# One f32 product in place of three f32r products in an encoder layer's projection, with the sample's experts chosen for both tiles together and the prompt's input normed beside it

## What is computed

```python
h = rmsnorm(x, g_mix)
proj  = h @ w_in                    # 3072 columns: q, k, v of branches A and B
gates = sigmoid(h @ w_gate + b_gate)   # 2048 columns
# A: windowed attention, 16 heads of 64;  B: dense attention, 8 heads of 128, q and k normed, rotary
x = x + (ga * (oa @ w_oa) + gb * (ob @ w_ob)) @ w_out
h = rmsnorm(x, g_ffn)               # then, for each token, 8 heads of:
qry = h @ w_query                   # 2 halves of 128 a head
s_top, i_top = top_k(qry . sub_keys, 16)       # for each half, over 128 keys
best, pos = top_k(s_top[0][:, None] + s_top[1][None, :], 16)
idx = i_top[0] * 128 + i_top[1] at pos;  g = softmax(best)
x = x + sum over the 128 chosen of  g * gelu(u[idx] . h) * v[idx]    # u, v: 16384 experts
y = rmsnorm(x, g_final)
```

## Time and profile before

| | us |
|---|---|
| median of 3 runs | 4944.76 (4940.06 to 4950.62) |
| the profiled execution, its time | 4939.81 |
| the profiled execution, span from first to last instruction | 4937.9 |
| PE busy, PEld | 3098.5 (63%), 1782.3 (36%) |
| DVE busy, ACT, POOL | 3340.8 (68%), 1042.4 (21%), 1728.8 (35%) |
| mean granted clock of TensorE | 0.739 |
| moved by DMA | 1568.77 MB, 318 GB/s |

### The profile page before, as it was taken

How to read it: one execution, slowest core, us unless ns; L and a number is a source line. 1 busy time by engine, 2 the same in 40 slices (tenths; PEclk the granted TensorE clock), 3 DMA queues, 4 the chain that set the end, 5 groups by cost and what they waited for, 6 DMA issues and landing times.

```text
span 4937.9 us, 72225 instructions
## 1 busy us (share of the span) xinstructions
PE 3098.5 (63%) x27052; PEld 1782.3 (36%) x27052; DVE 3340.8 (68%) x7744; ACT 1042.4 (21%) x2853; POOL 1728.8 (35%) x1393
## 2 busy tenths in 40 slices
PE   7686389885999989955545455445455444454433
PEld 6545367663777744432212112122122122121000
DVE  4426777786888866658867767667667577677554
ACT  3311111221555521111121121111211211211111
POOL 0200033323344323224444444444444444444443
PEclk9897699987999999966656666666566566565555
DMA  6143288897445477689999999999999999999998
GB/s 238 62 165 113 95 325 330 330 341 283 165 150 190 156 310 280 245 315 385 389 401 393 393 404 394 389 404 403 406 389 389 402 392 392 394 391 383 407 392 326
DMA packets 281852, 1568.77 MB, mean 318 GB/s; under 512 B 28064, under 2 KB 48032, under 8 KB 112928
## 3 DMA queue, kind: packets, MB, share of 16 engines
q0 software_dynamic: 184320, 1342.26, 68.9%
q1 hardware_dynamic: 97184, 221.90, 12.1%
...
## 4 chain that ended last, share of the span: by engine, by line
DMA 32%; issue 7%; PE 7%; DVE 5%; POOL 4%; ACT 2%; another core or an unknown queue 0%; POOLq 0%; DVEq 0%; SPq 0%; ACTq 0%
DMA prompt_exp_ring<-in_experts_dram,prompt_exp_idx 29%; PE prompt_exp_acc L1966 6%; POOL prompt_exp_ring L1619 4%; DVE prompt_exp_junk L1864 3%; DMA prompt_exp_ring<-in_experts_dram,prompt_exp_idx_all 3%; ACT prompt_exp_diag L1696 2%; PE prompt_exp_qp L1927 1%; DVE prompt_exp_pos L1743 0%; DVE prompt_exp_best L1739 0%; PE prompt_exp_qp L1987 0%; DVE prompt_exp_dot L1864 0%; DMA prompt_exp_wq<-in_w_query_dram 0%; DVE prompt_exp_crest L1748 0%; DVE prompt_exp_topi L1743 0%
## 5 line engine op out<-in xcount | busy, mean ns | idle before, releaser
L1966 PE MATMUL prompt_exp_acc<-prompt_exp_ring,prompt_exp_diag 32*32 32x512 f32 x16384 | 936.3, 940 | 1396.1 <-ACT prompt_exp_diag L1696 1395.3
L1864 DVE CUSTOM_DVE_ANT_0 prompt_exp_junk<-prompt_exp_ring,prompt_exp_h_now 128x1024 bf16<-128x1024 f32 x1024 | 1244.9, 1227 | 698.3 <-DMA prompt_exp_ring<-in_experts_dram,prompt_exp_idx 654.0
L1619 POOL DMA_INDIRECT prompt_exp_ring<-in_experts_dram,prompt_exp_idx x896 | 1032.0, 1152 | 1369.8 <-PE prompt_exp_acc L1966 1205.3
L1966 PEld LDWEIGHTS prompt_exp_acc<-prompt_exp_ring,prompt_exp_diag 32*32 32x32 f32 x16384 | 168.6, 127 | 1948.6 <-issue 1945.9
L1690 ACT ACTIVATE prompt_exp_ge<-prompt_exp_dot 128x2 f32<-128x2 f32 x512 | 104.1, 203 | 2286.8 <-DVE prompt_exp_dot L1864 2286.6
L144 POOL DMA_INDIRECT bg_ring<-in_experts_dram,bg_idx x128 | 175.1, 1368 | 667.2 <-DVE bg_acc L180 367.3
L1927 PEld LDWEIGHTS prompt_exp_qp<-prompt_exp_hT,prompt_exp_wq 128*128 128x128 f32 x2048 | 314.6, 243 | 144.7 <-issue 141.8
L1927 PE MATMUL prompt_exp_qp<-prompt_exp_hT,prompt_exp_wq 128*128 128x128 f32 x2048 | 338.1, 334 | 4.2 <-DMA prompt_exp_wq<-in_w_query_dram 2.4
L283 POOL DMA_INDIRECT sample_hid_ring<-in_experts_dram,sample_hid_idx x128 | 131.8, 1030 | 512.7 <-DVE sample_hid_acc L313 496.0
L703 PE MATMUL prompt_proj_acc<-prompt_proj_w_hi,prompt_proj_hT_hi 128*128 128x512 f32 x640 | 261.1, 408 | 27.0 <-ACT prompt_proj_w_hi L596 23.1
L1696 ACT ACTIVATE prompt_exp_diag<-prompt_exp_fold,prompt_exp_wgt 128x32 f32<-128x32 f32 x1024 | 264.4, 306 | 0.4 <-issue 0.2
...
## 6 DMA issues: line engine op xcount, KB each, us to landing
...
```

The costliest lines, as they stand in the source:

```text
L1619: nc.gpsimd.indirect_dma_start(out=ring[:, s % RING, :], out_offset=None, in_=experts, in_offset=bass.IndirectOffsetOnAxis(ap=column(s), a ...
L1864: nc.vector.tensor_tensor_reduce(out=junk[:, s % 2, :], in0=ring[:, s % RING, 0:D], in1=h_now[:], scale=1.0, scalar=0.0, op0=ALU.mult, op1 ...
L1966: last = nc.tensor.matmul(acc[at:at + Q, rows, :], diag[k, (g - 1) % 2, c, :], ring[k, s % RING, D + half * 512:D + half * 512 + 512], sta ...
```

## The change

The three f32r products of the projection become one product in f32, so the splits and their buffers go. The norm of x stands in a function of its own, `phase_norm`, and is used for the sample, which now asks for six chunks of weights in it and not three. `Background` is gone; tile 0 of the sample is done by `Hidden` with a ring of 8 under the prompt's projection, where VectorE leaves all copies out of PSUM to ScalarE (`SIDES` is 1). The sample's choice of experts gets a stage of its own, `phase_query`: each step takes one head for both tiles (a query product has 256 columns), and beside it the prompt's eight tiles are loaded, squared (ScalarE), scaled in two passes (GpSimd), transposed (TensorE) and copied to `hT_next` (ScalarE); the first three weight chunks are loaded, too. `phase_project` of the prompt is `given` both and has no norm. The core of the diff:

```diff
-        NR, NHI, NLO, RB = (1, 2, 1, 1) if bg else (3, 3, 3, 2)
-        AHEAD = NHI - 1
-        hT_hi, hT_lo = m.sb("hT_hi", [P, KD, nt * P], F32R), m.sb("hT_lo", [P, KD, nt * P], F32R)
...
+                load_weights(sp)
...
+def phase_project(nc, sems, tag, nt, x, g_mix, w_all, ident_d, proj, rope, k_norm_g, state_d, given=None, bg=None):
+    with ExitStack() as ctx:
+        m = Mem(nc, ctx, sems, tag)
+        NL, RB, SIDES = (CHUNKS_AHEAD, 1, 1) if bg else (6, 2, 2)
+        hT, w = given or (m.sb("hT", [P, KD, nt * P]), m.sb("w", [P, NL, KD, CW]))
+        THERE = NL if given else 0
+        ident = m.sb("ident", [P, P])
+        eps = m.sb("eps", [P, 1])
+        const_ld, eps_set = m.sem("const_ld"), m.sem("eps_set")
+        w_ld = [m.sem(f"w_ld{b}") for b in range(NL)]
+        wv = w_all.rearrange("(k p) c -> p k c", p=P)
+        def load_w(sp, c):
+            at = ORDER[c] * CW
+            sp.dma_start(w[:, c % NL, :, :], wv[:, :, at:at + CW]).then_inc(w_ld[c % NL], 16)
+        if not given:
+            phase_norm(nc, sems, tag, nt, x, g_mix, ident_d, ident, eps, const_ld, eps_set, hT,
+                       lambda sp: [load_w(sp, c) for c in range(NL)])
...
                 for u in range(UNITS):
                     c, t = divmod(u, nt)
-                    sp.wait_ge(staged[u % 2], u // 2 + 1)
+                    sp.wait_ge(staged[u % SIDES], u // SIDES + 1)
                     at = ORDER[c] * CW
                     sp.dma_start(proj[t * P:(t + 1) * P, at:at + CW], stage[:, u % SG, :]).then_inc(stored[u % SG], 16)
-                    if t == 0 and c + NR < CHUNKS:
-                        sp.wait_ge(w_lo_ready, c + 1)
-                        load_w(sp, c + NR)
+                    if t == 0 and c and c - 1 + NL < CHUNKS:
+                        sp.wait_ge(mm_tile, c * nt)
+                        load_w(sp, c - 1 + NL)
...
-                if u % 2 == side:
+                if u % SIDES == side:
...
                 for u in range(UNITS):
                     c, t = divmod(u, nt)
                     leave(act, nc.scalar.copy, u, 0)
-                    if t == SPLIT_AT and c + AHEAD < CHUNKS:
-                        split(c + AHEAD)
-                    if (p := bg_pair(u)) is not None:
-                        bg.gelu(act, At(0, SLOTS, 0), 2 * p)
+                    if bg:
+                        plan.act(bg, act, u)
...
+                        plan.dve(bg, dve, u)
...
                 for u in range(UNITS):
                     c, t = divmod(u, nt)
                     if t == 0:
-                        large(u, True, False)
-                        large(u + 1, True, False)
-                        small(u, False, True)
-                    elif t == nt - 1 and t > 1:
-                        small(u, True, False)
-                        large(u, False, True)
-                    else:
-                        if t > 1:
-                            large(u, True, False)
-                        small(u, False, True)
+                        if c >= THERE:
+                            pe.wait_ge(w_ld[c % NL], 16 * ((c - THERE) // NL + 1))
+                    if u >= 4:
+                        pe.wait_ge(staged[u % SIDES], (u - 4) // SIDES + 1)
+                    for k in range(KD):
+                        last = nc.tensor.matmul(acc[:, u % 4, :], hT[:, k, t * P:(t + 1) * P], w[:, c % NL, k, :],
+                                                start=(k == 0), stop=(k == KD - 1))
+                    last.then_inc(mm_tile, 1)
...
+def phase_query(nc, tag, x2, g_ffn, w_query, sub_keys, ident_d, iota_d, kept, x_next, g_mix, first_ds, hT_next, w_first):
...
+                for i in range(B):
+                    sp.dma_start(xn[:, i, :], x2[i * P:(i + 1) * P, :]).then_inc(xn_ld, 16)
+                sp.dma_start(gffn[:], g_ffn.broadcast_to([P, D])).then_inc(gain_ld, 16)
+                sp.dma_start(ident[:], ident_d).then_inc(ident_ld, 16)
+                load_wq(0)
+                for dst, src in ((keys[:], sub_keys), (iota[:], iota_d.broadcast_to([P, TOPK]))):
+                    sp.dma_start(dst, src).then_inc(const_ld, 16)
+                load_wq(1)
+                sp.dma_start(gmix[:], g_mix.broadcast_to([P, D])).then_inc(gain_ld, 16)
+                load_x(0)
+                load_x(1)
+                for i in range(B):
+                    sp.wait_ge(h_ready, i + 1)
+                    sp.dma_start(kept[0][i * P:(i + 1) * P, :], h_[:, i, :]).then_inc(kept_stored, 16)
...
+                for h in range(HEADS):
+                    if h % 2 == 1 and h // 2 + 2 < HEADS // 2:
+                        sp.wait_ge(q_full, h + 1)
+                        load_wq(h // 2 + 2)
+                    if h + 2 < PT_:
+                        sp.wait_ge(t_transposed, h + 1)
+                        load_x(h + 2)
+                for c, first_d in enumerate(first_ds):
+                    sp.dma_start(w_first[:, c, :, :], first_d).then_inc(first_ld, 16)
...
+                pool.wait_ge(gain_ld, 32)
+                def scale(t):
+                    x = xt[:, t % 2, :]
+                    pool.wait_ge(scaled2, t + 1)
+                    nc.gpsimd.tensor_scalar(x, x, stat2[:, 2, t:t + 1], None, ALU.mult).then_inc(normed2, 1)
+                    pool.wait_ge(normed2, t + 1)
+                    nc.gpsimd.tensor_tensor(x, x, gmix[:], ALU.mult).then_inc(ht_ready, 1)
+                for t in range(PT_):
+                    scale(t)
...
+                act.wait_ge(eps_set, 1)
+                for i in range(B):
+                    norm(i)
+                act.wait_ge(summed, B)
+                nc.scalar.activation(stat[:, 1, :], stat[:, 0, :], ACT.Sqrt, bias=eps[:], scale=1.0 / D).then_inc(root, 1)
+                for i in range(B):
+                    act.wait_ge(h_transposed, i + 1)
+                    nc.scalar.copy(hT[:, :, i * P:(i + 1) * P], tp[:, i, :].rearrange("p (k c) -> p k c", c=P)).then_inc(hT_ready, 1)
+                spread_q(0)
+                square(0)
+                square_root(0)
+                for h in range(HEADS):
+                    if h + 1 < HEADS:
+                        spread_q(h + 1)
+                    if h + 1 < PT_:
+                        square(h + 1)
+                        square_root(h + 1)
+                    spread_t(h)
+                act.wait_ge(best_ready, 1)
+                nc.scalar.activation(soft[:], soft[:], ACT.Exp).then_inc(exp_ready, 1)
...
+                def choose(h):
+                    dve.wait_ge(s_full, h + 1)
+                    top16([(top[:, i, p, :], topi[:, i, p, :], sc[:, h % 2, i, p, :], rest[:, i, p, :]) for i in each for p in range(2)])
+                    dve.sem_inc(s_free, 1)
+                    nc.vector.tensor_copy(topf[:], topi[:])
+                    for i in each:
+                        last = nc.vector.tensor_tensor(cand[:, i, :].rearrange("p (a b) -> p a b", a=TOPK),
+                                                       top[:, i, 0, :].unsqueeze(2).to_broadcast([P, TOPK, TOPK]),
+                                                       top[:, i, 1, :].unsqueeze(1).to_broadcast([P, TOPK, TOPK]), ALU.add)
+                    link(last)
+                    top16([(best[:, i, h, :], pos[:, i, :], cand[:, i, :], crest[:, i, :]) for i in each])
...
+                dve.wait_ge(gain_ld, 32)
+                dve.wait_ge(root, 1)
+                link(nc.vector.reciprocal(stat[:, 2, :], stat[:, 1, :]))
+                for i in each:
+                    nc.vector.scalar_tensor_tensor(h_[:, i, :], xn[:, i, :], stat[:, 2, i:i + 1], gffn[:], ALU.mult, ALU.mult).then_inc(h_ready, 1)
+                dve.wait_ge(const_ld, 32)
+                invert(0)
+                for h in range(HEADS):
+                    choose(h)
+                    if h + 1 < PT_:
+                        invert(h + 1)
...
+                def transpose_t(t):
+                    pe.wait_ge(ht_ready, t + 1)
+                    if t >= 2:
+                        pe.wait_ge(t_copied, t - 1)
+                    for k in range(KD):
+                        last = nc.tensor.transpose(tp[:, t % 2, k * P:(k + 1) * P], xt[:, t % 2, k * P:(k + 1) * P], ident[:])
+                    last.then_inc(t_transposed, 1)
...
+                query(0)
+                pe.wait_ge(const_ld, 32)
+                for h in range(HEADS):
+                    scores(h)
+                    if h + 1 < HEADS:
+                        query(h + 1)
+                    transpose_t(h)
...
-    mix(sample, 0, ST, True)
     sems = []
-    with ExitStack() as back:
-        bg = Background(nc, Mem(nc, back, sems, "bg"), sample[4], experts, g_final)
-        project(prompt, bg, sample[3][3], sample[3][4])
-    release(nc, sems)
-    with Hiding(sample, 1) as hidden:
+    with ExitStack() as normed:
+        m = Mem(nc, normed, sems, "normed")
+        given = m.sb("hT", [P, KD, PT_ * P]), m.sb("w", [P, CHUNKS_AHEAD, KD, CW])
```

(6 more changed lines are left out.)

392 lines of the change are left out of this document (184 added, 208 removed).

## The result

| | before | after |
|---|---|---|
| median of 3 runs, us | 4944.76 (4940.06 to 4950.62) | 4894.19 (4885.91 to 4897.19) |
| ratio of after to before | | 0.9897, 95% interval 0.9882 to 0.9912 |
| the profiled execution, its time and span | 4939.81, 4937.9 | 4894.19, 4892.3 |
| mean granted clock | 0.739 | 0.751 |

What follows compares the result with a forecast made beforehand. No engine was taken to be full; TensorE waits for the engines that split its weights. Terms +11.8, +12.6 and -59.2 sum to -34.8 us, taking the median from 4944.76 to 4910 us, 8-in-10 range 4892 to 4946.

Steps and rivals of the forecast that it cites:

- The f32 product: Both projections: a unit of 16 records takes 6.87 us in f32, against 5.60 us in f32r.
- The sample's projection: First stage: 173.3 us instead of 161.52, +11.8 us, with TensorE starting at 27.1 us behind SP's six loads.
- Rival (c): Sample's projection: SP doesn't hold the first block and PE starts at 20.2 us; 4903 us, chance 0.12.
- The start of the choice: Sample's choice of experts: waiting for gmix and the first query make the start 20.8 us later.
- The choices: Sample's choice of experts: 8 steps of 16.5 us, 132.0 us instead of 143.0, -11.0 us.
- The end of the stage: Sample's choice of experts: softmax, table load and four stores take 8.2 us instead of 5.35, +2.8 us.
- GpSimd free: Choice of experts: GpSimd's passes, done 5 us into each choice, cost VectorE 0; upper bound 38 us.
- The prompt's projection: Fourth stage: -46.0 us before the first product and -13.2 us from there on, together -59.2 us.
- Rival (b): Prompt's projection: late rows stop PSUM copies, TensorE's clock falls to 0.92, +47.8 us; 4958 us, chance 0.13.
- Rival (d): Choice of experts: TensorE waits for transposed prompt tiles, half of the norm's 42 us returns; 4931 us, chance 0.08.
- Sum: Whole kernel: the three changed stages together save 34.8 us, for a median of 4910 us.
- the prompt's products and what follows them: Prompt's projection from its first product to attention: 573.6 us instead of 586.8, -13.2 us.

Runs made afterwards that it cites:

- e3_three: Changed kernel, with the sample's norm asking for three weight chunks and the other three asked for in the next block; 4887.32 us, ratio 0.9886.
- e1_gain: Changed kernel, with VectorE's norm of the sample waiting for the gain gffn alone and only GpSimd for gmix; 4882.27 us, ratio 0.9880.
- e6_links: Changed kernel with the eight semaphore increments a step of the kernel before put back in the choice; 4902.18 us, ratio 0.9925.
- e5_third: Changed kernel with a third, unused GpSimd pass behind the two over each prompt tile; 4908.10 us, ratio 0.9926.
- e8_ring2: Changed kernel with a ring of 2 instead of 8 under the prompt's projection; that stage took 1261 us (575.2 with eight), no total time given.
- e9_projonly: Changed kernel with the sample's experts chosen by the old stage and the prompt's norm in its projection; 4939.59 us, ratio 1.0002 to before.

## Why the prediction was right, and where not

- *The f32 product, 6.87 us a unit:* right, 13.73 us for two units stored.
- *The sample's projection, +11.8:* right, +12.2, and for the reason given: TensorE's first product at 27.03 us (27.1 forecast), SyncE held for 23.98. Rival (c) fell, and `e3_three` showed what it would have brought.
- *The start of the choice:* the wait for `gmix` was forecast to end 22.4 us into the stage and ended at 23.1, the first MAX8 was forecast at 41.07 and came at 41.03. Its reason holds (`e1_gain`). The first query was put at some 9.5 us, 5.3 of them at half speed; it took 9.32. That it matched is in part luck, since the same code gave 7.17 us in another execution.
- *The choices:* this is the term that was mis-sized. Forecast 132.0 us, measured 123.9 (439.50 to 563.40): the step was taken from the old steps of two heads, 16.83, less 0.5 for casts and 0.2 more for a reciprocal. It is 15.48. `e6_links` puts 0.84 of the 1.0 down to semaphore increments, which the old step has and the new one doesn't. Both kernels' code shows it. The forecast took off what the profile counts as busy, the casts, and not the increments, which it doesn't count.
- *The end of the stage:* 8.2 forecast, 6.5 measured (563.40 to 569.92). The forecast had a table load of 1.28 us in it, and the exp came without one, as it had in the kernel before.
- *GpSimd free:* right, by 0.01 us, and so by luck. I had taken 2.36 us for its tensor_scalar; it is 2.85, and `cand` comes at 5.5 us and not at 5.8. The two errors ate the margin of 0.8 us that the forecast had. `e5_third` shows the cliff behind it.
- *The prompt's projection, -59.2:* -57.8, with the clock at 0.99 and VectorE at the 366 us that were forecast. ScalarE is at 101: the forecast's "about 100" was near, though its own terms (103, forty more copies of 0.6, ten casts of 3.6 less) make 91. Rival (b) did not come about; it appears with one row in flight (`e8_ring2`) and not with a ring of four. Rival (d) fell: steps are 15.48 with the norm beside them and 15.42 without.
- *Sum:* -34.8 against -43.8 at the border of the last stage. Of the 9.0 between them 8.1 are the choices and 1.7 their end; the other terms are off by 1.4 or less each and nearly cancel. What the medians' 50.6 has beyond 43.8 is put down to scatter: against nine later executions of the kernel before, five of the changed one were 42.8 us faster.

The forecast had the prompt's products and what follows them 13 us shorter, against 12 us lost in the sample, and the measured stages agree: in `e9_projonly` the part from the first product on is 12.3 us shorter and the sample's projection 11.0 longer. But the loads that come with them cost the norm another 3 us, so the new projections alone are no gain at all. The gain is the norm's move, 33 us, and the choice for both tiles, 11.
